# A hybrid Hyena and attention layer: half of the second branch's product moved into the long convolution, and the convolution's forward banks made a ring of two

## The reference, cut to what matters

```python
y_a = _hyena(zx[..., :OFF_Q], ...)               # order-2 long convolution, width 512
y_b = _window_attention(q, k, v, kc, vc, sink)   # width 512
ga, gb = jnp.split(jax.nn.sigmoid(gate_logits), 2, axis=-1)
merged = (ga * (y_a @ w_branch_a) + gb * (y_b @ w_branch_b)) @ w_out
x_new = x + g1 * merged
```

## Time and profile before

| what | value |
|---|---|
| time, median of 3 runs | 2344.74 us (2344.73 to 2345.3) |
| the profiled execution's own time | 2345.9 us |
| its span, first to last instruction | 2344.0 us |
| TensorE busy, share of the span | 2162.7 us, 92% |
| VectorE, ScalarE busy | 1677.2 us (72%), 1125.6 us (48%) |
| mean granted TensorE clock | 0.961 of full speed |
| convolution, first to last instruction | 774.3 to 945.1 us |
| merge, the 16 tiles of both branches on TensorE | 945.6 to 1056.7 us |
| output projection, norm and router after them | 1056.7 to about 1179 us |

### The profile page before, as it was taken

How to read it: one execution, slowest core, us unless ns; L and a number is a source line. 1 busy time by engine, 2 the same in 40 slices (tenths; PEclk the granted TensorE clock), 3 DMA queues, 4 the chain that set the end, 5 groups by cost and what they waited for, 6 DMA issues and landing times. The chain is left out here.

```text
span 2344.0 us, 27007 instructions
## 1 busy us (share of the span) xinstructions
PE 2162.7 (92%) x10004; PEld 1696.4 (72%) x10004; DVE 1677.2 (72%) x1726; ACT 1125.6 (48%) x1140; POOL 165.3 (7%) x51
## 2 busy tenths in 40 slices
PE   6699999979989787999919999999999999999998
PEld 1598888866658676447718888888888888888886
DVE  2528755147744698345588898888988888898886
ACT  3412212146500100011117777877777777777774
POOL 0000000010000000000000111101111110111100
PEclk9799999989989898999959999999999999999999
DMA  6333355130020003424349999999999999999993
GB/s 238 90 101 108 125 172 187 47 126 15 15 81 1 36 18 126 145 90 162 113 179 337 362 378 377 378 393 391 376 378 377 376 382 389 391 376 376 378 375 115
DMA packets 176026, 532.01 MB, mean 227 GB/s; under 512 B 14752, under 2 KB 52780, under 8 KB 175445
## 3 DMA queue, kind: packets, MB, share of 16 engines
q1 hardware_dynamic: 166800, 501.48, 57.2%
q0 software_dynamic: 4608, 16.78, 2.7%
q10 hardware_dynamic: 4548, 12.80, 1.4%
HBM read 497.47 MB, written 33.55 MB: 227 GB/s over the span
## 5 line engine op out<-in xcount | busy, mean ns | idle before, releaser
L2024 DVE TENSOR_TENSOR r_lo<-ring,r_hi 128x2048 fp32r<-128x2048 f32 x384 | 872.1, 2290 | 104.7 <-ACT r_hi L1983 102.9
L1983 ACT ACTIVATE r_hi<-ring 128x2048 fp32r<-128x2048 f32 x384 | 731.4, 1915 | 197.2 <-PE p_b L465 75.5
L463 PE MATMUL p_a<-r_hi,x_hi 128*128 128x512 f32 x512 | 203.3, 397 | 4.3 <-DVE x_lo L2035 4.3
L463 PE MATMUL p_y<-r_hi,a_hi 128*128 128x512 f32 x512 | 205.5, 401 | 0.0
L465 PE MATMUL p_a<-r_hi,x_lo 128*128 128x512 f32 x512 | 200.4, 391 | 0.0
L465 PE MATMUL p_y<-r_hi,a_lo 128*128 128x512 f32 x512 | 200.2, 391 | 0.0
L464 PE MATMUL p_a<-r_lo,x_hi 128*128 128x512 f32 x512 | 200.0, 391 | 0.0
L464 PE MATMUL p_y<-r_lo,a_hi 128*128 128x512 f32 x512 | 199.4, 389 | 0.0
L463 PE MATMUL p_b<-r_hi,x_hi 128*128 128x512 f32 x512 | 199.2, 389 | 0.0
L464 PE MATMUL p_b<-r_lo,x_hi 128*128 128x512 f32 x512 | 199.2, 389 | 0.0
L465 PE MATMUL p_b<-r_hi,x_lo 128*128 128x512 f32 x512 | 199.2, 389 | 0.0
(11 more groups left out here) (293 smaller groups left out, 3515.8 us busy)
## 6 DMA issues: line engine op xcount, KB each, us to landing
ring<-in_w_gate SPq DMA_DIRECT2D x128, 1024.0 KB, 9.2
ring<-in_w_up SPq DMA_DIRECT2D x128, 1024.0 KB, 9.1
ring<-in_w_down SPq DMA_DIRECT2D x128, 1024.0 KB, 12.2
w_raw<-in_w_in SPq DMA_DIRECT2D x17, 1024.0 KB, 6.0
ada_rest<-in_ada_w SPq DMA_DIRECT2D x16, 1024.0 KB, 5.4
ada<-in_ada_w SPq DMA_DIRECT2D x4, 2048.0 KB, 17.2
gate_dram<-zs ACTq DMA_DIRECT2D x16, 512.0 KB, 2.7
x_normed<-gate_dram SPq DMA_DIRECT2D x16, 512.0 KB, 4.3
```

What stands on the lines that cost most here:

```text
L463: pe.matmul(out, a_hi, b_hi, start=start, stop=False)
L1983: act.activation(r_hi[:, i % PARTS], ring[:, i % RAW], ACT.Copy).then_inc(hi_ready, 1)
L2024: dve.tensor_tensor(r_lo[:, i % PARTS], ring[:, i % RAW], r_hi[:, i % PARTS].bitcast(F32), ALU.subtract).then_inc(lo_ready, 1)
```

## The change

Two things are done together. **One:** the forward banks of the convolution become a ring of two banks. Every bank that `turn` or `forward` fills is numbered; ScalarE copies each one to SBUF (to `ut` or to `cp`, which now holds both banks of a part), and TensorE fills bank number `n` when `n - 2` is emptied. VectorE reads both operands from `cp`. It is now ScalarE that waits for VectorE's `x_read` before it overwrites `cp`, and TensorE no longer waits for it. **Two:** the two banks that this frees take the products of the second branch for the first 512 tokens, 8 of them (`branch(j)`), which TensorE makes at set places in the convolution; ScalarE copies each to `staged` and stores it to the new DRAM tensor `mb_dram`, one at a time. For them the first half of `y_b` (`y2`) and the weights (`w2`, two buffers of 128 columns) are loaded. In the merge the first 8 tiles have the first branch's product only, and the second one is loaded from `mb_dram` beside the gates. The gates of the convolution have one buffer in place of two.

```diff
@@ convolve @@
-        cp = sb("cp", [P, 2, 2, HC])
+        cp = sb("cp", [P, 2, 2, 2 * HC])
-        gate = sb("gate_in", [P, 2, 2, L])
-        pj = ps("p_j", [P, 2, 2, 512])
+        gate = sb("gate_in", [P, 2, L])
+        y2 = sb("yb_early", [P, NCH, 512])
+        w2 = sb("wb_columns", [P, 2, NCH, P])
+        staged = g["hid"]
+        pj = ps("p_j", [P, 2, 512])
+        p_b = ps("p_branch", [P, 2, 512])
...
+        through_banks = [("turn", 0), ("forward", 0), ("forward", 1), ("turn", 1), ("forward", 2), ("forward", 3),
+                         ("turn", 2), ("forward", 4), ("forward", 5), ("turn", 3), ("forward", 6), ("forward", 7)]
+        def first_bank(kind, i):
+            return 4 * through_banks.index((kind, i))
...
@@ SyncE @@
+                def load_columns(j):
+                    if j >= 2:
+                        sp.wait_ge(branch_done, j - 1)
+                    sp.dma_start(w2[:, j % 2], A["w_branch_b"][0][:, P * j:P * j + P].rearrange("(c p) n -> p c n", p=P))\
+                      .then_inc(w2_in[j % 2], 16)
+                def load_gate(i):
+                    if i:
+                        sp.wait_ge(gated, 2 * i)
...
+                def load_merge_input(i, tile, src):
                     sp.wait_ge(spec_ready, 2 * FC * (i + 1))
...
+                load_columns(0)
+                load_columns(1)
+                sp.dma_start(y2[:], g["yb_dram"][:, 0:512].rearrange("(c p) t -> p c t", p=P)).then_inc(y2_in, 16)
+                load_gate(0)
+                load_columns(2)
+                load_columns(3)
+                load_columns(4)
+                load_gate(1)
+                load_columns(5)
+                load_merge_input(0, g["yb"], g["yb_dram"])
+                load_gate(2)
+                load_columns(6)
+                load_merge_input(1, g["wa"], A["w_branch_a"][0])
+                load_gate(3)
+                load_columns(7)
+                load_merge_input(2, g["wb"], A["w_branch_b"][0])
@@ TensorE @@
                 def turn(i):
+                    if i >= 2:
+                        pe.wait_ge(gated, 2 * (i - 1))
                     for par in range(2):
-                        if i:
-                            pe.wait_ge(x_read, 2 * (2 * i - 1) + par + 1)
...
                         for q2 in range(2):
+                            n = first_bank("turn", i) + 2 * par + q2
+                            if n >= 2:
+                                pe.wait_ge(emptied, n - 1)
...
                 def forward(k):
...
-                            pe.wait_ge(x_read, 2 * (k - 1) + odd + 1)
...
+                            if c == 0:
+                                pe.wait_ge(emptied, max(first_bank("turn", i) + 4, n - 1))
+                            else:
+                                pe.wait_ge(emptied, n - 1)
...
+                def branch(j):
+                    if j == 0:
+                        pe.wait_ge(y2_in, 16)
+                    pe.wait_ge(w2_in[j % 2], 16 * (j // 2 + 1))
+                    if j >= 2:
+                        pe.wait_ge(branch_read, j - 1)
+                    for c in range(NCH):
+                        mm = pe.matmul(p_b[:, j % 2], w2[:, j % 2, c, :], y2[:, c, :], start=c == 0, stop=c == NCH - 1)
+                    mm.then_inc(branch_done, 1)
...
                 turn(1)
+                branch(0)
+                branch(1)
+                branch(2)
                 forward(2)
                 back(0)
                 forward(3)
                 back(1)
+                branch(3)
                 turn(2)
                 forward(4)
                 back(2)
                 forward(5)
                 back(3)
+                branch(4)
                 turn(3)
...
                 back(5)
+                branch(5)
                 back(6)
+                branch(6)
+                branch(7)
                 back(7)
@@ ScalarE (the calls stand in TensorE's order) @@
+                def transformed(k):
                     for odd in range(2):
...
+                        for bank in range(2):
+                            n = first_bank("forward", k) + 2 * odd + bank
+                            act.wait_ge(filled, n + 1)
+                            if k:
+                                act.wait_ge(x_read, 2 * (k - 1) + odd + 1)
+                            act.activation(cp[:, odd, bank], pj[:, n % 2], ACT.Copy).then_inc(emptied, 1)
+                def branch(j):
+                    act.wait_ge(branch_done, j + 1)
+                    if j:
+                        act.wait_ge(branch_stored, 16 * j)
+                    act.activation(staged[:], p_b[:, j % 2], ACT.Copy).then_inc(branch_read, 1)
+                    act.wait_ge(branch_read, j + 1)
+                    act.dma_start(g["mb_dram"][P * j:P * j + P, :], staged[:]).then_inc(branch_stored, 16)
@@ VectorE, spectral @@
-                        dve.wait_ge(cp_ready, 2 * k + odd + 1)
-                        other = pj[:, odd, 1].rearrange("p (z n) -> p z n", z=2)
+                        dve.wait_ge(emptied, first_bank("forward", k) + 2 * odd + 2)
+                        one, other = (cp[:, odd, bank].rearrange("p (z n) -> p z n", z=2) for bank in range(2))
@@ merge @@
+        mb = step[:].rearrange("p (b n) -> p b n", b=2)
...
+                    if h == 0:
+                        sp.dma_start(mb[:, i % 2], g["mb_dram"][P * j:P * j + P, :]).then_inc(mb_in[i % 2], 16)
...
-                        for br, (w, y) in enumerate(((wa, ya), (wb, yb))):
+                        for br, (w, y) in enumerate(((wa, ya), (wb, yb))[:h + 1]):
...
-                    dve.tensor_tensor(tb[:, i % 2], gates[:, i % 2, 1], b[:, 1], ALU.mult).then_inc(read, 1)
+                    if i < KD:
+                        dve.wait_ge(mb_in[i % 2], 16 * (i // 2 + 1))
+                    second = mb[:, i % 2] if i < KD else b[:, 1]
+                    dve.tensor_tensor(tb[:, i % 2], gates[:, i % 2, 1], second, ALU.mult).then_inc(read, 1)
```

More of the change, by code:

```diff
@@ L161, in build @@
         g["yb_dram"] = nc.dram_tensor("yb_dram", [NH * HD, L], F32).ap()
+        g["mb_dram"] = nc.dram_tensor("mb_dram", [D, L // 2], F32).ap()
         g["xn2_dram"] = nc.dram_tensor("xn2_dram", [L, D], F32).ap()
@@ L1373, in convolve @@
         spec = sb("spec", [P, 2, 2, 2, 2, HC])
-        gate = sb("gate_in", [P, 2, 2, L])
-        pj = ps("p_j", [P, 2, 2, 512])
-        acc = ps("p_acc", [P, 2, 4, LQ])
-        gate_in = [sem(f"gate_in{i}") for i in range(2)]
-        t_job, x_job, b_done = sem("turn_job"), sem("x_job"), sem("back_done")
-        t_ready, cp_ready, x_read = sem("ut_ready"), sem("cp_ready"), sem("x_read")
+        gate = sb("gate_in", [P, 2, L])
[4 more added lines that the diff above has]
+        p_b = ps("p_branch", [P, 2, 512])
+        acc = ps("p_acc", [P, 2, 4, LQ])
+        gate_in = sem("gate_in")
+        y2_in, w2_in = sem("yb_early_in"), [sem(f"wb_columns_in{i}") for i in range(2)]
+        branch_done, branch_read, branch_stored = sem("branch_done"), sem("branch_read"), sem("branch_stored")
+        filled, emptied, b_done = sem("bank_filled"), sem("bank_emptied"), sem("back_done")
+        x_read = sem("x_read")
         step, spec_ready = sem("wave_step"), sem("spec_ready")
@@ L1465, in _, with turned @@
             def _(act):
-                for k in range(N):
-                    i, c = divmod(k, FC)
+                def turned(i):
                     for par in range(2):
[L1469 to L1472, removed]
-                    for odd in range(2):
[L1474 to L1478, removed]
+                        for q2 in range(2):
+                            n = first_bank("turn", i) + 2 * par + q2
+                            act.wait_ge(filled, n + 1)
+                            act.activation(ut[:, i % 2, par, q2].rearrange("p h n -> p (h n)"), pj[:, n % 2], ACT.Copy)\
+                               .then_inc(emptied, 1)
@@ new lines, in transformed @@
+                def transformed(k):
+                    for odd in range(2):
+                        for bank in range(2):
+                            n = first_bank("forward", k) + 2 * odd + bank
+                            act.wait_ge(filled, n + 1)
+                            if k:
[8 more added lines that the diff above has]
+                    act.dma_start(g["mb_dram"][P * j:P * j + P, :], staged[:]).then_inc(branch_stored, 16)
@@ new lines, in _ @@
+                turned(0)
+                transformed(0)
+                transformed(1)
+                turned(1)
+                branch(0)
+                branch(1)
+                branch(2)
+                transformed(2)
+                transformed(3)
+                branch(3)
+                turned(2)
+                transformed(4)
+                transformed(5)
+                branch(4)
+                turned(3)
+                transformed(6)
+                transformed(7)
+                branch(5)
@@ L1480, in _ @@
```

(6 more changed lines are left out.)

35 lines of the change are left out of this document (12 added, 23 removed).

## The result

The changed kernel takes 2313.04 us (median of 4 runs, 2311.77 to 2315.32), the kernel before beside it 2344.77. The ratio is 0.9865, 95% interval 0.9848 to 0.9882: 31.7 us faster. The forecast was 2311.4, range 2307.5 to 2316.5. Two further sets of runs of the same kernel gave 2312.61 and 2311.50, 32.7 and 33.7 us under the kernel before beside them. The profiled execution took 2311.77 us with a span of 2309.7, 34.3 us under the span before; 2312.6 and 2310.7 were forecast for these two.

What follows compares the result with a forecast made beforehand. VectorE was taken to set the convolution's pace, except where banks held TensorE back, and matmul count the merge's. 27.5 + 0.4 + 4.4 + 1.3 - 0.3 = 33.3 us off 2344.7 gives 2311.4 us, range 2307.5 to 2316.5.

Steps and rivals of the forecast that it cites:

- 8 groups leave the merge: Merge, first 8 tiles: each loses the second branch's 8 recorded matmuls, 8 x 3.44 = 27.5 us less.
- first turn, VectorE starts earlier: Convolution, `turn(0)`: at its end TensorE waits for one bank's copy, not two; 0.4 us gained.
- VectorE's waits before three gatings: Convolution: VectorE's waits of 1.79, 1.32 and 1.31 us before `gating` go; 4.4 us gained.
- last `back`: End of the convolution: `back(7)` takes 8.7 us after about 3.1 us idle; 1.3 us gained, bounds 0 and 2.9.
- merge's first group at low clock: Start of the merge: the first group stays at 5.17 us in place of 3.60, so nothing is gained.
- TensorE waits for the loads: Merge's first half: 0.3 us lost to loads, bounds 0 and 2.3; about 1 us if it starts at full clock.
- The margins of 2.1 and 2.7 us: Convolution, before `gating`: TensorE is 2.1 us early the first time and 2.7 us early in the next two sets.
- B: Convolution: TensorE is still late for `gating`, all three waits come back, +4.4 us: 2316 us; chance 0.10.
- C: Merge's first half: loads bound it at 4.85 us a tile, 2.0 us more lost: 2313.4, up to 2315; chance 0.12.
- D: TensorE's clock stays up: 1.6 us at `back(7)` and as much at the merge's start: 2308.2 us; chance 0.07.
- E: Convolution: the ring makes TensorE run at 1.2 GHz in all forwards, slower than before: 2360 us; chance 0.03.
- F: Convolution: the moved work isn't hidden and the 27.5 us come back: about 2344 us, no change; chance 0.02.

Runs made afterwards that it cites:

- branches_last2: Changed kernel with all 8 branch products after the last `back`, where nothing hides them, weights in three buffers; 2343.18 us, ratio 0.9991 to the kernel before.
- ring_only: Changed kernel with only the ring of two banks, both products staying in the merge; 2341.94 us, ratio 0.9986 to the kernel before.
- branch_before_back: Changed kernel with branch products 3, 4 and 5 one place earlier, ahead of the `back` that `gating` waits for; 2315.81 us.
- w_out_pieces: Changed kernel with `w_out` loaded in four 1 MB parts behind the gates of tiles 1 to 4, router weights behind tile 5's; 2311.75 us.
- ring_of_one: Changed kernel with TensorE waiting for the bank before the one it fills, so that it pauses at every bank; 2351.0 us.
- w_out_later: Changed kernel with the 4 MB load of `w_out` issued after the gates of tile 3 and not of tile 1; 2311.97 us.
- the best kernel: Changed kernel with `w_out` loaded in four parts and the last `gating` split to begin at half of the last `back`; 2307.82 us, again 2308.94.
- after_again: The changed kernel itself, unaltered, run a second time as a control; 2312.61 us, ratio 0.9861 to the kernel before.
- split_end: As w_out_later, and the last `gating` begins when the last `back` has done the first half of the channels; 2310.53 us.

## Why the prediction was right

| term | forecast | first profile after |
|---|---|---|
| 8 groups leave the merge | 27.5 | 27.5 |
| first turn, VectorE starts earlier | 0.4 | 0.3 (783.25 to 782.93) |
| VectorE's waits before three gatings | 4.4 | 4.6 from start to start: all gone, with their hand-overs; 0.1 given back by `spectral` at 16.97 |
| last `back` | 1.3 | 1.1 (9.95 to 8.86) |
| merge's first group at low clock | 0 | 1.6 |
| TensorE waits for the loads | -0.3 | -0.9 |
| all behind the 16 tiles | 0 | 0.2 |
| sum | 33.3 | 34.3 by the spans (the rounded terms give 34.4) |

**The move is worth what TensorE had idle.** Shown by branches_last2, which has the same products and takes back 30 us, 27.6 of them the products themselves, and by the busy time in the convolution, 24.4 us more at an unchanged VectorE. 27.5 us went into waits of 10.87, twice 3.64, 2.54 and 9.71 us.

**The ring takes TensorE's wait for VectorE away**, and with it VectorE's three waits. Shown by ring_only: 3.4 us by the medians against 4.8 forecast. The difference lies in the clock after `turn(3)`, in the first turn, which at low clock takes 3.71 us for 3.50, in `spectral` and in the last `back` (10.15 for 9.95). In the whole change the three waits went entirely, in the first profile; in the second one 0.30 us came back. ScalarE's busy time in the convolution rose by 15.1 us and not by 19, since a turn's two copies of 0.60 us stand in the place of one of 1.02. VectorE's additions are 40 and not 32; they took 0.68 us for 128x512 before and after, as I had it.

**The margins of 2.1 and 2.7 us** came out as 2.7 and twice 2.5: `back(1)` ended at 833.43, `gating(0)` began at 836.11. The second was partly luck. I had a turn at 3.4 us and left out the wait at its end; `turn(2)` took 2.7 and the wait 0.7. Behind `turn(1)` no `forward` waits, and there the shorter turn is most of the 0.6 us by which the first margin was too small. Moving a product of 3.44 us into them left waits of 0.70 to 1.73 us (branch_before_back). The second, 1.73, is more than the sum gives, because the turn before it took 3.56 us for 2.68 and its `forward` began late.

**The clock** was the term with the largest error. I counted a loss of 1.6 us at the last `back` and another of the same size at the merge's start, unchanged from before. In the first profile the loss is in the `back` (8.86) and not in the merge; in the second it is in the merge and not in the `back` (7.17). Each time it was one of the two. So the forecast gain lacked 1.6 us here. On the other side the wait for the loads cost 0.9 us, 0.3 in the sum; the prediction had said that it would be about 1 if the merge began at full clock, and that is what happened, at the place named, tile 6. The two errors cancel in part, which is also luck.

**The medians** lie at 2311.5 to 2313.0, all above the forecast of 2311.4. The forecast took the profiled execution's 1.2 us over the median as a fixed distance, while the runs of either kernel differ by more than this, and the profiled one after was the fastest of its four.

**The rivals.** B (late for `gating`): 0 to 0.3 us, not 4.4. C (loads): 0.9 us; w_out_pieces shows loads slower than TensorE, hidden by four tiles of lead. D (the clock stays up): half, one loss of two. E: refuted for the ring of two, whose `forward` takes 7.07 to 9.69 us; in the ring of one the clock fell behind turns with pauses of 0.69 us in them, not between banks of `forward`. (By its own sum E becomes slower than before when a `forward` takes over 11.9 us, not 11.5.) F: refuted, by the 31.7 us and by ring_only's idle times. The chances of my forecast, C, D and most of B add up to over 0.9, not to a little over 0.8.

## What to carry to other kernels

Independent matmuls can cost nothing if they stand behind the work that the pacing engine waits for, and in a place where TensorE would wait for that engine; one step ahead of it, they cost 0.7 to 1.7 us each here. When a resource (here banks) is released by the slow engine, a copy by an idle third engine frees it earlier, and that may be what makes room for the move. Where a big load stands in front of small ones that are needed every few microseconds, moving it only moves the wait; cut it into parts and put them between.

## What the runs showed that was not expected

- The same kernel has its clock fall at different places from one execution to the next, and in these profiles the later falls go with the first. Behind `turn(3)`, after 1.5 us idle and the turn, a `forward` took 7.17 or about 9.6 us. Where it took 7.17, the last `back` mostly had 2.86 us of idle time before it and took 8.86, and the merge began at full clock (the changed kernel's first and third profile, w_out_later and both of the best kernel). Where it took about 9.6 (after_again, w_out_pieces, split_end), the idle time was 2.21 us, the `back` took 7.17, and after 2.92 us idle the merge lost 1.6 us; only in split_end, with 1.79 us idle, it did not. In branch_before_back, where `back(6)` was slow in its place (8.63 us), the end went as in these. Why the first fall comes or stays away is open.
- This doesn't explain the runs' spread of 2 to 4 us. Both kinds of profile of the changed kernel take 247.9 to 248.4 us from the start of the convolution to the output projection, while that start itself lies between 774.18 and 775.51.
- In ring_of_one three banks of `forward` behind `turn(2)` ran at half clock although TensorE was busy 8.63 of 10 us in that stretch (866 to 876 us, clock 0.50); in 890 to 893, with pauses as long between banks of matmuls, it was 2.15 of 3 us busy and the clock stood at 1.00. The Trainium skill, TensorE: Matmul & The Clock Gate, "Part 4: PE-mode transpose", states that the full clock doesn't engage for transposes, which don't count as busy in the same way. The falls behind turns are in line with the second part. The first isn't so here: `turn(2)` of the changed kernel (838.5 to 841.2 us) ran at clock 1.00. No run tells transposes apart from the turns' shorter groups.
- Two loads behind 4 MB landed after 10.2 us (median) while 415 GB/s were moved. The stores of the products (256 KB each) landed after 2.0 us (median of 8); one of them nevertheless held ScalarE for 3.69 us before it copied `branch(2)`, at no cost.
